# A decoder layer with 32 experts on one core: expert 1's tokens are gathered before expert 0's last weight unit, and the final norm's weight comes by a transfer

## The chip, the cores and the metric

The kernel runs on one core of one Trainium2 chip. The metric is the device time of one execution in microseconds (us); the kernel before has a median of 1227.49 us over 3 runs. The engines that matter here are TensorE (PE, matrix products), VectorE (DVE), ScalarE (ACT), GpSimd (POOL), and SyncE (SP), whose only work is to issue DMA transfers.

## The reference

One layer, 256 tokens of width 1024, all in float32. What lies before the experts (norm, projection, two kinds of attention, merge) is not touched by the change. The part that is:

```python
x = x + merged @ w_out[layer]
hf = rmsnorm(x, norm_ffn_g[layer])
x = x + moe_ffn(hf, w_router[layer], b_router[layer], w1[layer], b1[layer], w2[layer], b2[layer])
return rmsnorm(x, norm_final_g)

# moe_ffn: each token goes to the top 4 of 32 experts
gu = xb @ w1[e] + b1[e]                       # 1024 -> 2048
gate = jnp.minimum(gu[:, :F], SWIGLU_LIMIT)
up = jnp.clip(gu[:, F:], -SWIGLU_LIMIT, SWIGLU_LIMIT)
act = (up + 1.0) * gate * jax.nn.sigmoid(SWIGLU_ALPHA * gate)
y = act @ w2[e] + b2[e]                       # 1024 -> 1024, then weighed and added to the token
```

## The kernel before, in words

**Stages.** Up to about 309 us the kernel computes the attention part and the residual `x2`. Then it routes the tokens, and from about 320 us it walks through the 32 experts. Each expert has room for 64 tokens (`CAP`).

**One expert.** The weights of an expert arrive in six units of 2 MB: four of `w1` (two of eight rows of 128 each) and two of `w2`. For each expert PE *gathers* its tokens (48 small products of the token parts `x_parts` with a 0/1 selection, into PSUM bank 2, L1263, and 6 products that gather the tokens' norm scales into bank 3, L1251). DVE then multiplies the two into `XT` (`store_scales` L1814, `store_x` L1819). PE multiplies `XT` with the four `w1` units (`hidden_unit`, L1289), adds a bias (L1299), and the sums lie in banks 0 and 1. DVE and ACT make the activation of them (`activate`: clamps L1890 and L1891, sigmoid on ACT L914, products L1899 and L1902). PE transposes it (L1336), multiplies with the two `w2` units (L1355), and scatters the result into banks 4 to 7 (L1444), which hold the residual from the start. In the loop each of these steps belongs to another expert, so that PE needs not wait: expert i+1's hidden units, then the gather for i+2, the scatter for i, and the `w2` units of i. The transposes of expert i's activation (`transpose_previous`) come behind the first hidden unit of expert i+1.

**The weight stream.** SP issues the transfers in one fixed order into a ring of ten units. Before it issues unit n it waits until PE has used unit n-9 (`s_used`, counted up at the end of each unit). So PE gives back the places, and DMA fills them.

**Expert 0** stands apart, in `hidden_first`, ahead of the loop. Its order on PE: unit 0, unit 1, unit 2, bias, the scales of expert 1 (`second_scales`), then `spread_gain`, then unit 3. `spread_gain` (L1470) multiplies rows of the final norm's weight with columns of the identity, so that banks 6 and 7 hold this weight in all 128 partitions. ACT copies it to the tile `gain` (L907). That tile is also `rest`, scratch space of POOL and ACT while they split `x2` in three bf16 parts (until `s_lo` is 4), so the copy can't be earlier; and banks 6 and 7 must be free again before ACT puts the second half of the residual there (L910, `s_res`). Behind unit 3 PE gathers expert 1's tokens, runs 8 filler products (`fill(3, 8)`) and waits for the residual and for `XT`. It can't gather earlier, as `XT` is one tile: DVE may overwrite it with expert 1's tokens only when unit 3 has read expert 0's.

**The end.** Behind the last unit and the last scatter ACT sums squares (L942, L944), and DVE multiplies with the root and with `gain` (L1966, wait on `s_gain`) and SP stores the result (L633).

Of the kernel before, what the change touches and what calls it, by code (L numbers as in the profile page):

```python
# [7 lines left out]
ALU = mybir.AluOpType  # L8
# [101 lines left out]
def hybrid_block_kernel(nc, x_in, g_mix, w_in, rel_bias, w_att, w_ret, w_out, g_ffn, w_router, b_router,  # L110
                        w1, b1, w2, b2, g_final, c_early, c_lasting, c_decay, c_onehot, c_mask, c_item,
                        c_expert, out):
    with ExitStack() as ctx:
# [3 lines left out]
        def sem(name):  # L117
            return ctx.enter_context(nc.semaphore(name))
# [4 lines left out]
        def bank(b, n=1):  # L123
            return psf[:, b * HALF:(b + n) * HALF]
# [101 lines left out]
        ul = A_W[:, 5632:6144]  # L226
        sg = A_W[:, 6144:6656]
        act_sb = gl
        s_w = A_W[:, 6656:6912].rearrange("p (t s) -> p t s", t=TT)
        sc_w = A_W[:, 6912:7168]  # L230
        actT = A_W[:, 7168:7680]
# [147 lines left out]

        s_pair = [sem(f"ring_pair_loaded{j}") for j in range(RING // 2)]  # L380
        s_unit = [sem(f"w1_unit_of_first_or_last_or_extra_loaded{u}") for u in range(W1_UNITS)]
        s_gainp = sem("final_gain_in_psum")
        s_used = sem("ring_units_used")
        s_xfirst = sem("first_rows_of_first_tokens_stored")
        s_extra2 = [sem(f"extra_w2_loaded{u}") for u in range(W2_UNITS)]
# [133 lines left out]
        def _(sp):  # L519
# [96 lines left out]
            for j in range(W2_ROWS):  # L616
                flat = place(N_UNITS - 1)[0]
                sp.dma_start(w2_tile(flat)[:, j, :], w2_source(N_EXP - 1, 1)[:, j, :]).then_inc(s_quarter[j], 16)

            sp.wait_ge(s_used, N_UNITS)  # L620
            sp.wait_ge(s_table, 1)
            n = sp.value_load(list_i[0:1, 0:1], min_val=0, max_val=MAX_EXTRA)
# [15 lines left out]
        def _(pool):  # L638
# [34 lines left out]
            def low_part(m):  # L673
                t, h, cols = HALVES[(2, 3, 0, 1)[m]]
                pool.wait_ge(s_mid, m + 1)
                pool.tensor_tensor(x_part(2, t)[:, cols], rest[:, h], x_part(1, t)[:, cols], ALU.subtract)\
                    .then_inc(s_lo, 1)
# [16 lines left out]
            rest_part(1)  # L694
            low_part(2)
            low_part(3)
            pool.wait_ge(s_res, 2 * TT)
            pool.memset(sc_w, 0.0).then_inc(main.swe, 1)
            pool.memset(y_sb, 0.0).then_inc(main.ye, 1)

# [1 line left out]
        def _(act):  # L703
# [77 lines left out]
                          w_router.rearrange("(u p j) e -> p u j e", p=P, j=PAIR_ROWS)).then_inc(s_small, 16)  # L781
            act.dma_start(br_sb[:, :], bass.AP(b_router.tensor, 0, [[0, P], [1, N_EXP]])).then_inc(s_small, 16)
            act.dma_start(item_sb[:, :], c_item).then_inc(s_small, 16)
            act.dma_start(g_rows[:, :], g_final.rearrange("(c p) -> c p", p=P)).then_inc(s_grows, 16)
            act.dma_start(expert_sb[:, :], c_expert).then_inc(s_small, 16)
            with nc.allow_non_contiguous_dma(reason="1024 words, off the critical path"):
                act.dma_start(g_col[:, :].rearrange("p (u j) -> p u j", j=PAIR_ROWS),
# [112 lines left out]
            for t in range(TT):  # L900
                act.activation(gexp[:, t, :], top[:, 8 * t:8 * t + 4], ACT.Exp, bias=lowest[:, t, :],
                               accum_out=gden[:, t:t + 1]).then_inc(s_tke, 1)
            for t in range(TT):
                if t:
                    act.wait_ge(s_gainp, 1)
                    act.wait_ge(s_lo, 2 * TT)
                    act.activation(gain[:, :], bank(6, 2), ACT.Copy).then_inc(s_gain, 1)  # L907
                    act.wait_ge(s_gain, 1)
                for h in range(2):
                    act.activation(by_row_pair(bank(4 + 2 * t + h))[:, 0], in_row_pairs(x2[:, t, h * HALF:(h + 1) * HALF])[:, 0],  # L910
                                   ACT.Copy).then_inc(s_res, 1)
            def sigmoid(s, i):
                act.wait_ge(s.g, i + 1)
                act.activation(sg, gl, ACT.Sigmoid, scale=ALPHA).then_inc(s.sig, 1)  # L914
# [3 lines left out]
                act.activation(actT, bank(2), ACT.Copy).then_inc(s.ate, 1)  # L918

            act.activation(warm, warm, ACT.Sigmoid)  # L920
            sigmoid(main, 0)
            store_act(main, 0)
            with act.Fori(0, N_EXP - 2) as i:
                act.activation(warm, warm, ACT.Sigmoid)
# [24 lines left out]
        def _(pe):  # L949
# [330 lines left out]
                        scales.then_inc(main.gathered, 1)  # L1280
                mm.then_inc(main.gathered, 1)

            def hidden_unit(flat, u, row_done=None):
                tile = w1_tile(flat)
                for j in range(W1_ROWS):
                    k = u * W1_ROWS + j
                    for c in range(4):
                        o = ps[CAP * (c % 2):CAP * (c % 2) + CAP, c // 2, :]
                        mm = pe.matmul(o, XT[:, k, :], hidden_columns(tile[:, j, :], c),  # L1289
                                       start=(k == 0), stop=(k == KC - 1))  # L1290
                    if j == 0 and row_done is not None:
                        mm.then_inc(row_done, 1)
                return mm

            def hidden_bias(s, i):
                pe.wait_ge(s.sel1, i + 1)
                for c in range(4):
                    o = ps[CAP * (c % 2):CAP * (c % 2) + CAP, c // 2, :]
                    pe.matmul(o, sel1[0:BIAS_ROWS, :], hidden_columns(bias[:, 0:2 * F], c), start=False, stop=False)  # L1299

            def hidden_first():

                pe.wait_ge(s_xfirst, 1)
                for u in range(W1_UNITS):
                    pe.wait_ge(s_unit[u], 16)
                    if u == 1:
                        pe.wait_ge(main.x, 1)
                    hidden_unit(first_units[u], u, s_wu if u < HALF_UNITS else None).then_inc(s_used, 1)
                    if u == 2:
                        hidden_bias(main, 0)  # L1310
                        second_scales()
                        spread_gain()

            def hidden(i, first, rounds, behind_first_unit):

# [148 lines left out]
                pe.wait_ge(main.slots, 2)  # L1464
                gather_scales().then_inc(main.gathered, 1)

            def spread_gain():
                pe.wait_ge(s_grows, 32)
                for c in range(KC):
                    mm = pe.matmul(psf[:, 6 * HALF + c * P:6 * HALF + (c + 1) * P],  # L1470
                                   ident[0:KC, c:c + 1].broadcast_to([KC, P]), g_rows[:, :], start=(c % 4 == 0),
                                   stop=True, skip_group_check=True)
                mm.then_inc(s_gainp, 1)

            fill(0, 6)
            gather_first()
            fill(0, 6)
            pe.wait_ge(s_bias, 12)
            hidden_first()
            pe.wait_ge(s_lo, 2 * TT)  # L1480
            gather(main, 1, scaled=True)
            pe.wait_ge(main.scales, 2)
            fill(3, 8)
            pe.wait_ge(s_res, 2 * TT)
            with pe.Fori(0, (N_EXP - 2) // TURN) as r:
                rounds = r * (16 * TURN * E_UNITS // RING)
                for k in range(TURN):
# [28 lines left out]
        def _(dve):  # L1516
# [307 lines left out]
            for n, rows in enumerate((slice(0, W1_ROWS), slice(W1_ROWS, KC))):  # L1824
                count = rows.stop - rows.start
                scaled = dve.tensor_tensor(scale_rows[:, rows, :], scale_row.broadcast_to([P, count, CAP]),
                                           gain_of_row[:, rows, :], ALU.mult)
                if n:
                    scaled.then_inc(main.scales, 1)
                    dve.wait_ge(main.scales, 1)  # L1830
                else:
                    link(scaled)
                    dve.wait_ge(main.gathered, 2)
                dve.tensor_tensor(XT[:, rows, :], bank(2).rearrange("p (k s) -> p k s", k=KC)[:, rows, :],
                                  scale_rows[:, rows, :], ALU.mult).then_inc(main.x if n else s_xfirst, 1)
            choose_bias(sel1, main.sel1, 0)
            choose_bias(sel2, main.sel2, 0)
# [48 lines left out]
            def down_done(i):  # L1886
                dve.wait_ge(s_used, i * E_UNITS + W1_UNITS + E_UNITS)

            def activate(s, i, stored=None, scaled=False):
                dve.tensor_scalar(gl, bank(0), LIMIT, None, ALU.min).then_inc(s.g, 1)  # L1890
                dve.tensor_scalar(ul, bank(1), LIMIT, -LIMIT, ALU.min, ALU.max).then_inc(s.chain, 1)  # L1891
                if stored is not None and not scaled:
                    dve.wait_ge(s.x, stored)
                    store_scales(s, stored, scale_rows)
                dve.wait_ge(s.chain, i * 2 + 1)
                dve.wait_ge(s.g, i + 1)
                if stored is not None:
                    store_x(s, stored, scale_rows)
                dve.scalar_tensor_tensor(ul, ul, 1.0, gl, ALU.add, ALU.mult).then_inc(s.chain, 1)  # L1899
                dve.wait_ge(s.chain, i * 2 + 2)  # L1900
                dve.wait_ge(s.sig, i + 1)
                dve.tensor_tensor(act_sb.rearrange("s (j p) -> s j p", j=W2_ROWS),  # L1902
                                  ul.rearrange("s (p j) -> s j p", j=W2_ROWS),
                                  sg.rearrange("s (p j) -> s j p", j=W2_ROWS), ALU.mult).then_inc(s.act, 1)
# [5 lines left out]
                dve.wait_ge(s.sw, i + 1)  # L1910
                dve.tensor_copy(sc_w, ps[:, 2, 0:T]).then_inc(s.swe, 1)

            dve.wait_ge(s_res, 2 * TT)
            store_scales(main, 1, scale_rows)
            dve.wait_ge(s_used, W1_UNITS)
            activate(main, 0, 1, scaled=True)
            choose_bias(sel1, main.sel1, 1)
            slots(main, 2, 2)
            with dve.Fori(0, N_EXP - 2) as i:
                gated_slots(main, i, i, i)  # L1920
                hidden_done(i + 1)
                activate(main, i + 1, i + 2)
                choose_bias(sel1, main.sel1, i + 2)
                slots(main, i + 3, i + 3)
                store_scatter(main, i)
                down_done(i)
                store_y(main, i)
                choose_bias(sel2, main.sel2, i + 1)
# [13 lines left out]
            with dve.If(n > 0):  # L1942
# [15 lines left out]
                    store_y(extra, i)  # L1958
                dve.wait_ge(s_scattered, n + N_EXP + 1)
                dve.memset(lists[0:1, 64:65], 0.0)  # L1960
            dve.wait_ge(s_gain, 1)
            for n, (t, h, cols) in enumerate(HALVES):
                if h == 0:
                    dve.wait_ge(s_root, TT + t + 2)
# [33 lines left out]
```

## Time and profile before

| | us |
|---|---|
| median of 3 runs (lowest 1227.3, highest 1229.3) | 1227.49 |
| the profiled execution | 1227.92 |
| its span | 1225.9 |
| PE busy | 1169.0 (95%) |
| DVE busy | 428.0 (35%) |
| ACT busy | 207.7 (17%) |
| POOL busy | 58.5 (5%) |

The span is the time from the first to the last instruction of the profiled execution; what lies around it is 1227.92 - 1225.9 = 2.02 us. DMA moved 461.79 MB, 377 GB/s over the span. The granted clock of PE was 0.999 of full speed. PE is busy nearly all the time, but it isn't the only limit: the slices of the page show that DMA is at 400 GB/s and more over two thirds of the span.

### The profile page before, as it was taken

Reading aid. Unit: us, or ns where it says so; the run is one execution under the profiler, and the core shown is the slowest. Engines: PE = TensorE matmul, PEld = TensorE weight load, DVE = VectorE, ACT = ScalarE, POOL = GpSimd, SP = SyncE. Lnnn points to the kernel's source line nnn. Section 1 sums busy time; section 2 is a strip of 40 time slices with the busy share of each in tenths; the row PEclk is TensorE's granted clock in tenths of the full one; section 3 lists DMA queues with packets and bytes.
Section 4 is the critical chain, followed back from the end, with each engine's and each line's share of the span. In section 5 each row is a group of like instructions: output and inputs, shape, how many; then the busy total and the mean of one; then the engine's idle time right before and its main releaser. Section 6 shows DMA issues by size and latency. Waiting matters only on the chain.

```text
span 1225.9 us, 17199 instructions
## 1 busy us (share of the span) xinstructions
PE 1169.0 (95%) x7154; PEld 588.0 (48%) x7154; DVE 428.0 (35%) x741; ACT 207.7 (17%) x306; POOL 58.5 (5%) x43
## 2 busy tenths in 40 slices
PE   9999999999999999999999999999999899999897
PEld 8888888888643334333333333333333333333332
DVE  5886764655632223222222222222222222222222
ACT  6444553534400000000000000000000000000001
POOL 0850000000300000000000000000000000000000
PEclk9999999999999999999999999999999999999999
DMA  9756437877889999999999999999999999999996
GB/s 310 272 207 217 161 138 258 317 283 320 337 350 428 431 433 433 429 431 434 433 430 430 433 433 432 429 433 434 432 429 433 433 433 428 433 433 434 428 423 255
DMA packets 47522, 461.79 MB, mean 377 GB/s; under 512 B 4985, under 2 KB 6978, under 8 KB 32290
## 3 DMA queue, kind: packets, MB, share of 16 engines
q1 hardware_dynamic: 44760, 458.97, 89.9%
q10 hardware_dynamic: 2730, 2.36, 0.7%
q8 instruction: 24, 0.39, 0.1%
q14 instruction: 8, 0.07, 0.0%
HBM read 459.19 MB, written 1.07 MB: 375 GB/s over the span
## 4 chain that ended last, share of the span: by engine, by line
PE 66%; DMA 32%; DVE 1%; SPq 1%; ACT 0%; issue 0%; DVEq 0%; ACTq 0%
PE ps L1289 19%; DMA w_ring<-in_w 19%; PE ps L1355 12%; DMA A_QK<-in_w 6%; DMA xb_and_att<-in_w 6%; PE ps L1006 4%; PE ps L1444 4%; PE ps L1014 3%; PE ps L1012 3%; PE ps L1013 3%; PE ps L1263 2%; PE ps L1007 2%; PE ps L1026 1%; PE ps L1139 1%; PE ps L1141 1%; PE ps L1140 1%
## 5 line engine op out<-in xcount | busy, mean ns | idle before, releaser
L1289 PE MATMUL ps<-w_ring,A_W 128*64 128x512 f32 x1216 | 272.5, 596 | 28.9 <-DMA w_ring<-in_w 28.4
L1890 DVE TENSOR_SCALAR A_W<-ps 128x512 f32<-128x512 f32 x32 | 22.1, 692 | 478.2 <-PE ps L1289 478.2
L1289 PEld LDWEIGHTS ps<-w_ring,A_W 128*64 128x64 f32 x1216 | 84.8, 137 | 200.9 <-issue 160.2
L1355 PE MATMUL ps<-w_ring,A_W 128*64 128x512 f32 x608 | 137.9, 595 | 0.0
L1534 DVE TENSOR_TENSOR w_parts<-w_ring,w_parts 128x1024 fp32r<-128x1024 f32 x76 | 109.9, 1463 | 56.4 <-ACT w_parts L733 55.5
L1289 PE MATMUL ps<-A_QK,A_W 128*64 128x512 f32 x416 | 93.2, 595 | 9.3 <-DMA A_QK<-in_w 9.3
L918 ACT ACTIVATE A_W<-ps 128x512 f32<-128x512 f32 x31 | 18.5, 597 | 462.9 <-PE ps L1336 462.9
L1289 PE MATMUL ps<-xb_and_att,A_W 128*64 128x512 f32 x384 | 86.2, 596 | 9.4 <-DMA xb_and_att<-in_w 9.4
L733 ACT ACTIVATE w_parts<-w_ring 128x1024 fp32r<-128x1024 f32 x75 | 78.9, 1058 | 64.6 <-PE ps L1007 32.1
L914 ACT ACTIVATE A_W<-A_W 128x512 f32<-128x512 f32 x32 | 20.2, 631 | 359.8 <-DVE A_W L1890 359.8
L1006 PE MATMUL ps<-hT_both,w_parts 128*128 128x512 f32 x224 | 79.3, 399 | 0.0
L1355 PEld LDWEIGHTS ps<-w_ring,A_W 128*64 128x64 f32 x608 | 41.5, 136 | 70.5 <-issue 69.0
L1012 PE MATMUL ps<-w_parts,hT_both 128*128 128x512 f32 x176 | 69.6, 396 | 0.0
L1014 PE MATMUL ps<-w_parts,hT_both 128*128 128x512 f32 x176 | 68.6, 390 | 0.0
L1013 PE MATMUL ps<-w_parts,hT_both 128*128 128x512 f32 x176 | 68.5, 389 | 0.0
L1444 PE MATMUL ps<-A_W 64*128 64x512 f32 x264 | 65.9, 616 | 0.0
L1007 PE MATMUL ps<-hT_both,w_parts 128*128 128x256 f32 x224 | 62.9, 281 | 0.0
L1289 PEld LDWEIGHTS ps<-A_QK,A_W 128*64 128x64 f32 x416 | 29.3, 137 | 68.1 <-issue 59.7
L1289 PEld LDWEIGHTS ps<-xb_and_att,A_W 128*64 128x64 f32 x384 | 26.3, 137 | 64.3 <-issue 47.8
L1907 DVE COPY A_W<-ps 128x512 f32<-128x512 f32 x31 | 21.4, 692 | 98.0 <-PE ps L1355 98.0
L1263 PE MATMUL ps<-route,x_parts 128*128 128x64 bf16 x1488 | 48.5, 193 | 0.0
L1006 PEld LDWEIGHTS ps<-hT_both,w_parts 128*128 128x128 f32 x224 | 42.1, 188 | 11.1 <-issue 0.6
(266 smaller groups left out, 1198.7 us busy)
## 6 DMA issues: line engine op xcount, KB each, us to landing
w_ring<-in_w SPq DMA_DIRECT2D x110, 2048.0 KB, 35.2
A_QK<-in_w SPq DMA_DIRECT2D x38, 2048.0 KB, 35.1
xb_and_att<-in_w SPq DMA_DIRECT2D x35, 2048.0 KB, 35.2
w_ring<-in_w_in SPq DMA_DIRECT2D x36, 1024.0 KB, 7.3
w_ring<-in_w SPq DMA_DIRECT2D x8, 1024.0 KB, 23.7
w_ring<-in_w_ret_branch SPq DMA_DIRECT2D x2, 2048.0 KB, 10.9
xb_and_att<-in_w SPq DMA_DIRECT2D x4, 1024.0 KB, 20.6
A_W<-in_w_out SPq DMA_DIRECT2D x1, 2560.0 KB, 13.0
```

The costliest lines, as they stand in the source:

```text
L733: act.activation(hi, raw, ACT.Copy).then_inc(s_wh, 1)
L1006: pe.matmul(o, wh, tokens_both(k), start=first, stop=False, skip_group_check=True)
L1007: mm = pe.matmul(o[:, 0, :], wl, hT_hi[:, k, :], start=False, stop=last, skip_group_check=True)
L1012: pe.matmul(bank(b + t), hh, hi, start=first, stop=False)
L1013: pe.matmul(bank(b + t), hh, lo, start=False, stop=False)
L1014: mm = pe.matmul(bank(b + t), hl, hi, start=False, stop=last)
L1263: mm = pe.matmul(ps[:, 2, k * CAP:(k + 1) * CAP], row_columns(x_part(part, t), k), s_one[:, t, :], start=(part == 0 and t == 0), stop=(par ...
L1289: mm = pe.matmul(o, XT[:, k, :], hidden_columns(tile[:, j, :], c), start=(k == 0), stop=(k == KC - 1))
L1355: mm = pe.matmul(ps[CAP * c:CAP * c + CAP, 3, :], lhs, w2_tile(flat)[:, q % W2_ROWS, c * HALF:(c + 1) * HALF], start=False, stop=(q == FQ ...
L1444: mm = pe.matmul(bank(4 + 2 * t + c), weights[rows, t * P:(t + 1) * P], y[rows, :], start=False, stop=True, skip_group_check=True)
L1534: dve.tensor_tensor(lo, raw, hi.bitcast(F32), ALU.subtract).then_inc(s_wl, 1)
L1890: dve.tensor_scalar(gl, bank(0), LIMIT, None, ALU.min).then_inc(s.g, 1)
```

## The change

1. The sums of expert 0's hidden layer go to banks 6 and 7 (`FIRST_BANK = 6`) instead of 0 and 1, and its tokens lie in `XT_first`, which is the place of `gl`, instead of `XT`.
2. PE gathers expert 1's tokens before unit 3 of expert 0. DVE stores its scales and its tokens at once, without waiting for the residual, and chooses bias and slots of the experts that follow before it clamps expert 0's sums.
3. `spread_gain` and its row transfer go. SP loads `gain` with one transfer of 128 copies of the row (512 KB), issued behind the last weights.
4. The filler products behind expert 0 go. ACT puts the second half of the residual in banks 6 and 7 after the sigmoid of expert 0, when DVE has read both banks. PE no longer waits for the residual; DVE does before it enters its loop. POOL clears `sc_w` one step earlier.

```diff
+        XT_first = gl.rearrange("p (k s) -> p k s", k=KC)
+        FIRST_BANK = 6
...
@@ sync, behind the last w2 quarter
+            sp.wait_ge(s_lo, 2 * TT)
+            sp.dma_start(gain[:, :], bass.AP(g_final.tensor, 0, [[0, P], [1, D]])).then_inc(s_gain, 16)
             sp.wait_ge(s_used, N_UNITS)
@@ gpsimd
+            pool.wait_ge(s_res, 2)
+            pool.memset(sc_w, 0.0).then_inc(main.swe, 1)
             pool.wait_ge(s_res, 2 * TT)
-            pool.memset(sc_w, 0.0).then_inc(main.swe, 1)
             pool.memset(y_sb, 0.0).then_inc(main.ye, 1)
@@ scalar
-            act.dma_start(g_rows[:, :], g_final.rearrange("(c p) -> c p", p=P)).then_inc(s_grows, 16)
...
-            for t in range(TT):
-                if t:
-                    act.wait_ge(s_gainp, 1)
-                    act.wait_ge(s_lo, 2 * TT)
-                    act.activation(gain[:, :], bank(6, 2), ACT.Copy).then_inc(s_gain, 1)
-                    act.wait_ge(s_gain, 1)
+            def store_residual(t):
                 for h in range(2):
                     act.activation(by_row_pair(bank(4 + 2 * t + h))[:, 0], in_row_pairs(x2[:, t, h * HALF:(h + 1) * HALF])[:, 0],
                                    ACT.Copy).then_inc(s_res, 1)
+            store_residual(0)
...
             act.activation(warm, warm, ACT.Sigmoid)
+            act.wait_ge(s_res, 2)
             sigmoid(main, 0)
+            act.wait_ge(main.chain, 1)
+            store_residual(1)
+            act.wait_ge(s_res, 2 * TT)
             store_act(main, 0)
@@ tensor (hidden_unit and hidden_bias take the first bank, b, and hidden_unit the tokens, x)
-                    hidden_unit(first_units[u], u, s_wu if u < HALF_UNITS else None).then_inc(s_used, 1)
+                    hidden_unit(first_units[u], u, s_wu if u < HALF_UNITS else None, FIRST_BANK, XT_first).then_inc(s_used, 1)
                     if u == 2:
-                        hidden_bias(main, 0)
+                        hidden_bias(main, 0, FIRST_BANK)
                         second_scales()
-                        spread_gain()
+                        pe.wait_ge(s_lo, 2 * TT)
+                        gather(main, 1, scaled=True)
...
             hidden_first()
-            pe.wait_ge(s_lo, 2 * TT)
-            gather(main, 1, scaled=True)
-            pe.wait_ge(main.scales, 2)
-            fill(3, 8)
-            pe.wait_ge(s_res, 2 * TT)
@@ vector
-                dve.tensor_tensor(XT[:, rows, :], bank(2).rearrange("p (k s) -> p k s", k=KC)[:, rows, :],
+                dve.tensor_tensor(XT_first[:, rows, :], bank(2).rearrange("p (k s) -> p k s", k=KC)[:, rows, :],
...
-            dve.wait_ge(s_res, 2 * TT)
+            dve.wait_ge(main.x, 1)
             store_scales(main, 1, scale_rows)
-            dve.wait_ge(s_used, W1_UNITS)
-            activate(main, 0, 1, scaled=True)
+            store_x(main, 1, scale_rows)
+            dve.wait_ge(s_used, W1_UNITS - 1)
             choose_bias(sel1, main.sel1, 1)
             slots(main, 2, 2)
+            dve.wait_ge(s_used, W1_UNITS)
+            activate(main, 0, b=FIRST_BANK)
+            dve.wait_ge(s_res, 2 * TT)
             with dve.Fori(0, N_EXP - 2) as i:
...
-            dve.wait_ge(s_gain, 1)
+            dve.wait_ge(s_gain, 16)
```

PE around expert 0, before. `A_ATT`, `w_ring` and `A_W` hold the four weight units, `x_parts` the tokens to be gathered, `ones_bf` is the filler.

```order
L1289 MATMUL ps<-A_ATT,A_W 64x512 x8
L1289 MATMUL ps<-w_ring,A_W 64x512 x16
L1299 MATMUL ps<-bias_sb,route 64x512 x4
L1251 MATMUL ps<-route,small 128x64 x6
L1470 MATMUL ps<-g_rows,lasting 128x128 x8
L1289 MATMUL ps<-A_W 64x512 x8
L1263 MATMUL ps<-route,x_parts 128x64 x48
L1197 MATMUL ps<-ones_bf 128x128 x8
```

And now:

```order
L1293 MATMUL ps<-A_ATT,A_W 64x512 x8
L1293 MATMUL ps<-w_ring,A_W 64x512 x16
L1303 MATMUL ps<-bias_sb,route 64x512 x4
L1255 MATMUL ps<-route,small 128x64 x6
L1267 MATMUL ps<-route,x_parts 128x64 x48
L1293 MATMUL ps<-A_W 64x512 x8
```

The eight products with `g_rows` and the eight fillers are gone, and the 48 of the gather stand ahead of unit 3; the loop follows directly behind it.

DVE at the same place, before. L1814 and L1819 store the scales and tokens of expert 1; L1890, L1891, L1899 and L1902 are the activation of expert 0; L1805 and L1800 choose bias and slots.

```order
L1814 TENSOR_TENSOR A_W<-ps,g_col 128x512
L1890 TENSOR_SCALAR A_W<-ps 128x512
L1891 TENSOR_SCALAR A_W<-ps 128x512
L1819 TENSOR_TENSOR A_W<-ps,A_W 128x512
L1899 SCALAR_TENSOR_TENSOR A_W<-A_W 128x512
L1902 TENSOR_TENSOR A_W<-A_W 128x512
L1805 TENSOR_SCALAR route<-lasting 96x64
L1800 TENSOR_SCALAR route<-lasting,A_PT 128x64 x2
```

And now:

```order
L1806 TENSOR_TENSOR A_W<-ps,g_col 128x512
L1811 TENSOR_TENSOR A_W<-ps,A_W 128x512
L1797 TENSOR_SCALAR route<-lasting 96x64
L1792 TENSOR_SCALAR route<-lasting,A_PT 128x64 x2
L1882 TENSOR_SCALAR A_W<-ps 128x512
L1883 TENSOR_SCALAR A_W<-ps 128x512
L1891 SCALAR_TENSOR_TENSOR A_W<-A_W 128x512
L1894 TENSOR_TENSOR A_W<-A_W 128x512
```

The tokens of expert 1 are stored ahead of the activation of expert 0 instead of in its middle, and so are the choices of bias and slots.

ACT at the same place, before: the residual's first half (L910), the copy of the gain (L907), the residual's second half, the load of the sigmoid's table, the sigmoid (L914), the store of the transposed activation (L918).

```order
L910 ACTIVATE ps<-A_W 128x2x128x2 x2
L907 ACTIVATE gain<-ps 128x1024
L910 ACTIVATE ps<-A_W 128x2x128x2 x2
L920 ACT_TABLE_LOAD
L920 ACTIVATE small<-small 128x1
L914 ACTIVATE A_W<-A_W 128x512
L918 ACTIVATE A_W<-ps 128x512
```

And now:

```order
L908 ACTIVATE ps<-A_W 128x2x128x2 x2
L920 ACT_TABLE_LOAD
L920 ACTIVATE small<-small 128x1
L914 ACTIVATE A_W<-A_W 128x512
L908 ACTIVATE ps<-A_W 128x2x128x2 x2
L918 ACTIVATE A_W<-ps 128x512
```

The residual's second half now stands between the sigmoid and the store.

## Rows read from the trace of the kernel before

**Rows 1.** The page's 40 slices of 30.6 us: DMA's rate.

```profile
GB/s 310 272 207 217 161 138 258 317 283 320 337 350 428 431 433 433 429 431 434 433 430 430 433 433 432 429 433 434 432 429 433 433 433 428 433 433 434 428 423 255
```

**Rows 2.** The chain of waits from 331 us: start, duration, what ran.

```profile
331.40 1.98 PE ps L1470 x16
333.38 3.58 PE ps L1289 x16
336.96 1.52 PE ps L1263 x48
...
338.61 0.70 DVE A_W L1819
...
339.45 3.65 PE ps L1289 x16
343.10 0.45 PE ps L1299 x4
```

**Rows 3.** Windows: stretch, length, busy time of PE, PEld, DVE, ACT, POOL, clock, DMA share, GB/s.

```profile
324.00:339.50 15.50, 14.97 (x132) 7.77 (x129) 9.77 (x34) 7.40 (x14) 2.58 (x4) 1.00 0.98 395
339.50:344.00 4.50, 4.50 (x24) 1.70 (x24) 2.46 (x7) 0.00 (x0) 0.00 (x0) 1.00 0.01 5
344.00:1211.00 867.00, 819.94 (x5214) 303.18 (x5212) 201.34 (x430) 42.98 (x96) 0.00 (x0) 1.00 1.00 430
```

**Rows 4.** The timeline of SP's issues from 330 us: start, time, line.

```profile
330.70 0.33 SPq L597 DMA_DIRECT2D w_ring<-in_w  x1
343.14 4.96 SPq L442 DMA_DIRECT2D w_ring<-in_w  x2
```

**Rows 5.** The chain of waits at one turn of PE's loop, and from 602 us on.

```profile
467.32 3.58 PE ps L1355 x16
470.90 3.43 PE ps L1289 x16
...
602.97 36.85 DMA w_ring<-in_w
...
1125.38 38.94 DMA xb_and_att<-in_w
...
1164.36 7.09 PE ps L1289 x32
...
1211.49 5.30 PE ps L1404 x24
...
1220.50 1.41 DVE xb L1966 x2
```

**Rows 6.** The timeline of DVE, POOL and ACT, 323 to 341 us.

```profile
323.71 2.15 DVE L1800 TENSOR_SCALAR route<-lasting,A_PT 128x64 bf16<-128x64 f32 x2
324.66 1.15 POOL L676 TENSOR_TENSOR x_parts<-gain,x_parts 128x512 bf16<-128x512 f32 x1
332.06 0.16 DVE L1873 CAST wr_sb<-wr_sb 1x16 int32<-1x16 f32 x1
334.47 1.12 ACT L910 ACTIVATE ps<-A_W 128x512 f32<-128x512 f32 x2
335.68 0.69 DVE L1814 TENSOR_TENSOR A_W<-ps,g_col 128x512 f32<-128x512 f32 x1 [3.46 <-ACT ps L910]
337.62 0.68 DVE L1891 TENSOR_SCALAR A_W<-ps 128x512 f32<-128x512 f32 x1
337.74 0.63 ACT L914 ACTIVATE A_W<-A_W 128x512 f32<-128x512 f32 x1 [0.63 <-DVE A_W L1890]
339.22 0.68 DVE L1899 SCALAR_TENSOR_TENSOR A_W<-A_W 128x512 f32<-128x512 f32 x1
339.93 1.07 DVE L1902 TENSOR_TENSOR A_W<-A_W 128x512 f32<-128x512 f32 x1
```

**Rows 7.** Windows at the end of the weight stream; the page's issues of `x`, KB each, us to landing.

```profile
1212.50:1213.00 0.50, 0.50 (x5) 0.14 (x2) 0.00 (x0) 0.00 (x0) 0.00 (x0) 1.00 0.10 41
xb<-in_x SPq DMA_DIRECT2D x4, 512.0 KB, 4.2
```

More of the change, by code:

```diff
@@ L381, in hybrid_block_kernel @@
         s_unit = [sem(f"w1_unit_of_first_or_last_or_extra_loaded{u}") for u in range(W1_UNITS)]
-        s_gainp = sem("final_gain_in_psum")
         s_used = sem("ring_units_used")
@@ L1281, in gather_first, with hidden_unit @@
                 mm.then_inc(main.gathered, 1)
-            def hidden_unit(flat, u, row_done=None):
+            def hidden_unit(flat, u, row_done=None, b=0, x=XT):
                 tile = w1_tile(flat)
@@ L1287, in hidden_unit @@
                     for c in range(4):
-                        o = ps[CAP * (c % 2):CAP * (c % 2) + CAP, c // 2, :]
-                        mm = pe.matmul(o, XT[:, k, :], hidden_columns(tile[:, j, :], c),
+                        o = ps[CAP * (c % 2):CAP * (c % 2) + CAP, b + c // 2, :]
+                        mm = pe.matmul(o, x[:, k, :], hidden_columns(tile[:, j, :], c),
                                        start=(k == 0), stop=(k == KC - 1))
@@ L1293, in hidden_unit, with hidden_bias @@
                 return mm
-            def hidden_bias(s, i):
+            def hidden_bias(s, i, b=0):
                 pe.wait_ge(s.sel1, i + 1)
                 for c in range(4):
-                    o = ps[CAP * (c % 2):CAP * (c % 2) + CAP, c // 2, :]
+                    o = ps[CAP * (c % 2):CAP * (c % 2) + CAP, b + c // 2, :]
                     pe.matmul(o, sel1[0:BIAS_ROWS, :], hidden_columns(bias[:, 0:2 * F], c), start=False, stop=False)
@@ L1465, in second_scales @@
                 gather_scales().then_inc(main.gathered, 1)
[L1467 to L1473, printed above, removed]
             fill(0, 6)
@@ L1887, in down_done, with activate @@
                 dve.wait_ge(s_used, i * E_UNITS + W1_UNITS + E_UNITS)
[L1889 to L1892, printed above, removed]
+            def activate(s, i, stored=None, b=0):
+                dve.tensor_scalar(gl, bank(b), LIMIT, None, ALU.min).then_inc(s.g, 1)
+                dve.tensor_scalar(ul, bank(b + 1), LIMIT, -LIMIT, ALU.min, ALU.max).then_inc(s.chain, 1)
+                if stored is not None:
                     dve.wait_ge(s.x, stored)
```

## The prediction

> **What bounds the kernel now.** I read the page's slices first, then the chain of waits, then windows around the first experts and at the end. The slices show three parts [rows 1]. Up to about 368 us DMA moves less than its best, 138 to 350 GB/s. From slice 13 to the last but one it stays at 423 to 434 GB/s, which is all that it reaches anywhere. A stream that is always full can't be shortened by making PE faster inside it. It can only be started earlier. So the question is where its last hole lies, and what ends it.
>
> The windows answer that [rows 3]. From 324 to 339.5 us the DMA share is 0.98. From 339.5 to 344.0 it is 0.01, a hole of 4.5 us less a last rest. From 344.0 to 1211.0 us it is 1.00 at 430 GB/s, without any hole. SP's issues say why [rows 4]: after the issue at 330.70 comes the next at 343.14, and that is the transfer which waits for PE's fifth used unit, the first hidden unit of expert 1. In the chain of waits this unit runs from 339.45 for 3.65 us, until 343.10 [rows 2]. The first bytes of the full stream move about 0.9 us behind the issue.
>
> Behind it the chain is PE alone until about 602 us and then alternates between transfers of 36.85 to 38.94 us and PE [rows 5]. That is the same stream seen from two sides: PE, which had a lead of some units, has used them up. The last wait for weights ends at 1164.36, and from there PE runs to the end. So everything from 344 to the end hangs on one time, the end of the first hidden unit of expert 1. What PE saves before it, up to the size of the hole, comes out at the end in full; what it saves behind it would not.
>
> **The change part by part.**
>
> *Spreading the gain on PE.* The chain gives it 1.98 us, 331.40 to 333.38, with PE the only engine in it and nothing beside it that PE would otherwise wait for [rows 2]. It goes: -1.98 us.
>
> *The gather before unit 3.* The gather costs 1.52 us wherever it stands (336.96 to 338.48 [rows 2]): 0 by itself. What changes is the stretch behind it. Now DVE starts on the tokens only when the gather ends (L1819, 338.61, 0.70 us), and hidden unit 0 of expert 1 begins at 339.45 [rows 2]. Between 338.48 and 339.45 PE runs only fillers or waits: 0.97 us. In the new order DVE does this beside unit 3. With the gain gone the gather runs from 331.40 to 332.92, unit 3 from there for 3.58 us to 336.50. DVE is ready for it: its work on the routing tables ends at 332.06 + 0.16 = 332.22, then the scales take 0.69 us and the tokens 0.70 us, so `XT` is there at about 333.9, 2.6 us before PE wants it [rows 2, 6]. The gather's own inputs are there too, though PE asks for them 5.6 us sooner than before: the low parts at 324.66 + 1.15 = 325.81, the slots at 323.71 + 2.15 = 325.86 [rows 6], against 331.40. So the stretch of 0.97 us goes: -0.97 us. In the kernel before, the scales waited for the residual (3.46 us idle, released by ACT's L910 [rows 6]); that wait goes with it, and cost PE nothing.
>
> *The entry into PE's loop.* The branch stood behind fillers and a wait of PE; now it follows unit 3 directly, with nothing between. At a turn of the loop the trace shows no gap: the down unit at 467.32 takes 3.58 us, and the next hidden unit starts at 470.90 [rows 5]. The first entry is another matter, since its code may not be there yet, and the trace hides it. It costs at least 0 and at most about the idle part of the 0.97 us, some 0.5 us. It is nearest to the loop's turn, so I take 0 and keep 0.5 for the range.
>
> *The activation of expert 0.* It is the new tight place. PE transposes the activation after one hidden unit and a bias, 3.65 + 0.45 = 4.10 us after hidden unit 0 begins [rows 2], and it now begins when unit 3 ends, 2.49 us sooner than before (339.45 - 336.96). Counted from the end of unit 3, DVE did the clamps until 338.30, at 1.34 us; then it waited for the gather and stored the tokens; then it did L1899 in 0.68 us and L1902 in 1.07 us [rows 6]. Without the tokens between: 1.34 + 0.68 + 1.07 and 0.1 between them = 3.19 us. The sigmoid is off this path, as it ended at 338.37, or 1.41 us [rows 6]. So it is ready 0.91 us before PE asks. The residual's second half (1.12 us on ACT [rows 6]) stands behind the sigmoid and delays neither it nor the products; it ends at about 1.41 + 1.12 = 2.5 us, and the store of the transposed activation comes behind the transposes at 4.10. Cost 0; if ACT's copies and DVE slow each other, up to 0.91 us is covered.
>
> *The places in PSUM and SBUF.* The products have the same shapes in other banks: 0. ACT's copy of the gain and the row transfer issued on ACT's queue were covered by waits of ACT: 0. POOL's clear of `sc_w` comes earlier, and was not late.
>
> *The gain's transfer.* It is issued on SP behind the last weights, and behind it SP has only the final stores. The weight stream ends at about 1213.0 (window 1212.5 to 1213.0, share 0.10 [rows 7]), and `gain` is first read at 1220.50 [rows 5]. Both move together. 512 KB took a median of 4.2 us from issue to landing for `x` [rows 7], and at 430 GB/s [rows 3] it takes 1.2 us of the stream. So it lands between 1214.2 and 1217.2 in the old clock, at least 3.3 us before it is wanted. The last weights are ahead of it in the queue, and the end of PE's last stretch starts at 1211.49 with 5.30 us of products [rows 5], so a slight overlap with the last quarter would not be felt either. Cost 0. A source of which one row is read 128 times is not in the trace; that is the second rival.
>
> A rule of the Trainium skill bears on it ("DMA: Bandwidth & Descriptors", section "Rules for kernel authors"): a leading zero-stride dimension of c copies confines a transfer to at most c engines, for c below 16. Here c is 128, so by the rule all 16 engines are used and the cost is 0 as taken; no row here shows such a transfer of this size.
>
> **The sum.** -1.98 - 0.97 = -2.95 us for the start of the first hidden unit of expert 1, so for SP's issue (343.14 to 340.19) and for the stream's start (344.0 to about 341.05). The old transfers still end at about 339.6, so the hole shrinks from about 4.4 to 1.45 us and doesn't close: none of the gain is cut off. By the profiled execution: 1227.92 - 2.95 = 1224.97 us. Its time is 0.43 above the median of the runs, so against the median 1227.49 it is 1224.54; I say 1224.6.
>
> **The rivals.**
>
> *Part of it is taken back at expert 1's start.* The first entry of the loop costs up to 0.5 us, or the activation comes later than the 0.91 us of cover, for instance by contention in PSUM between ACT's residual copy and DVE. For it: the cover is thin and nothing in the trace shows that entry uncovered. Against it: the sum above has every step from a row. Price 0.5 to 1.4 us: 1225.1 to 1226.0.
>
> *The transfer of the gain is late.* One mechanism: its 128 reads of one row run on one or few of the 16 engines, or are served one after the other. On one engine the 512 KB at 430 / 16 = 27 GB/s take 19.5 us, from about 1212.5 to 1232 in the old clock instead of 1220.5, so +11.5 - 2.95 = +8.6 us: about 1236. It decides from 1220.5 on, that is if it takes over 7.5 us, and is slower than before if it takes over 10.5 us. Against it: 128 partitions are written, as with `x`, whose 512 KB landed in 4.2 us.
>
> *The stream doesn't pass it on.* If DMA isn't the full stream that its share claims, the saved time could be lost at a later hole, and the time stays 1227.5. For it: only that 350 to 340 GB/s slices stand close by. Against it: share 1.00 over 867 us, and in that span PE's chain would move by the same 2.95 us too. The nearest thing to it is a slower rate after a longer queue, which no row shows.
>
> **How the numbers follow.** Forecast as summed, 0.73: 1224.0 to 1225.1 with the runs' own spread. Part taken back, 0.17. Not passed on, 0.06. Gain late, 0.04, of which nearly all is slower. About 0.2% (2.45 us) is what a measurement of this kernel can tell from no change; the forecast of 2.95 us is only 0.5 us beyond it, and the runs before spread over 2 us. So of the forecast's 0.73 I count 0.62 as faster and 0.11 as the same; with part taken back (0.02 faster, 0.15 same) and not passed on (0.05 same, 0.01 slower): faster 0.64, same 0.31, slower 0.05. The range holds the forecast and most of the first rival: 1223.5 to 1226.3.
>
> **What would show it.** In the profile after, the chain should have no g_rows products, the gather at about 331.4, unit 3 ending at about 336.5, hidden unit 0 of expert 1 starting there without idle time, the transposes at about 340.6 without a wait for DVE, SP's next issue at about 340.2, a hole in DMA of about 1.5 us, then share 1.00; the last wait for weights should end at about 1161.4, and the span should be about 1222.9. The forecast is wrong if PE waits between unit 3 and the loop, or in front of the transposes, if the last wait for weights moves by less than 2.4 us, or if the first of the final products waits for a transfer.

## The result, and the profile after

The changed kernel takes 1233.28 us (median of 6 runs, 1233.01 to 1233.74), the kernel before 1227.45 us in the same comparison. The ratio is 1.0044, with a 95% interval of 1.0032 to 1.0056: slower by 5.8 us, where 2.95 us less were forecast. The profiled execution took 1233.71 us, its span is 1231.7 us.

The start went as forecast. Here is the chain of waits after, from 331 us, and SP's issue that opens the full weight stream (compare [rows 2, 4]):

```profile
331.08 1.40 PE ps L1267 x48
332.48 7.02 PE ps L1293 x32
339.50 0.45 PE ps L1303 x4
```

```profile
339.54 4.95 SPq L443 DMA_DIRECT2D w_ring<-in_w  x2
```

Unit 3 of expert 0 and the first hidden unit of expert 1 are now one piece of 32 records without a gap, and SP issues at 339.54 instead of 343.14: 3.60 us sooner. The loss is behind it. The chain at the first turn of PE's loop, to be read beside 467.32 and 470.90 of [rows 5]:

```profile
463.71 3.58 PE ps L1360 x16
467.30 3.84 issue
471.14 1.97 PE ps L1293 x4
473.11 3.84 issue
476.95 4.55 PE ps L1293 x12
```

PE stands still twice, for 3.84 us each, and the profile knows nothing that it waits for ("issue"). Two such stalls, of 3.0 to 4.7 us, return at each of the five turns (the branches back; the loop runs six times). Here is PE's idle time before L1293 that is put down to issue, from the list of waits (total, times, longest; ten of the eleven times are those at the turns), and the instruction queue on the page (packets, MB, share of 16 engines):

```profile
PE ps L1293 <- issue: 38.0, 11, 4.7
```

```profile
q8 instruction: 69, 1.13, 0.4%
```

The same row on the page of before:

```profile
q8 instruction: 24, 0.39, 0.1%
```

Between 470 and 1180 us the trace of before has no packet on this queue at all, and the trace after has 44. Here is the queue of the weights (q1) in this stretch, before, and then the queues of weights and instructions after:

```profile
q1 hardware_dynamic: 11798, 306.44, 100.3%
```

```profile
q1 hardware_dynamic: 11710, 304.47, 99.9%
q8 instruction: 44, 0.72, 0.4%
```

An instruction packet is 1.13 MB / 69 = 16 KB. The last wait for weights ends at 1170.16 instead of 1164.36 [rows 5], though the stream began 3.60 us sooner; so the stream lost 9.4 us on its way:

```profile
1131.18 38.93 DMA xb_and_att<-in_w
...
1170.16 7.09 PE ps L1293 x32
```

From there to the end both kernels need the same 61.54 us (1231.7 - 1170.16 and 1225.9 - 1164.36), so the tail with the gain's transfer cost nothing. And this is how the stream ends (windows of 1 us; the last two columns are DMA's share and GB/s), first before, then after:

```profile
1208.00:1209.00 1.00, 1.00 (x10) 0.46 (x10) 0.94 (x2) 0.00 (x0) 0.00 (x0) 1.00 1.03 410
1211.00:1212.00 1.00, 1.00 (x8) 0.29 (x6) 0.00 (x0) 0.00 (x0) 0.00 (x0) 1.00 0.50 197
1212.00:1213.00 1.00, 1.00 (x8) 0.34 (x6) 0.00 (x0) 0.00 (x0) 0.00 (x0) 1.00 0.18 74
```

```profile
1208.00:1209.00 1.00, 1.00 (x8) 0.25 (x4) 0.98 (x1) 0.00 (x0) 0.00 (x0) 1.00 0.97 397
...
1212.00:1213.00 1.00, 1.00 (x8) 0.35 (x6) 0.00 (x0) 0.69 (x2) 0.00 (x0) 1.00 0.50 205
1216.00:1217.00 1.00, 1.00 (x6) 0.30 (x4) 0.00 (x0) 0.00 (x0) 0.00 (x0) 1.00 0.52 213
1218.00:1219.00 1.00, 1.00 (x8) 0.30 (x6) 0.00 (x0) 0.00 (x0) 0.00 (x0) 1.00 0.27 111
```

For 9 us after, the share is one half and the rate one half; before, the end takes about 3 us in all. I read this as half of the 16 engines having finished while the other half lag behind; the trace doesn't name the engine of a packet.

### The profile page after: what moved, and what is told of

Same layout as the page of the kernel before. It is cut to its first block, busy times and chain, and to the rows that moved or that the text cites. A ratio compares the mean times of both kernels' runs of the same rounds, so it can differ in the third digit from the quotient of the medians.

```text
span 1231.7 us, 17151 instructions
## 1 busy us (share of the span) xinstructions
PE 1175.6 (95%) x7130; PEld 592.7 (48%) x7130; DVE 427.2 (35%) x741; ACT 206.6 (17%) x305; POOL 58.1 (5%) x43
## 3 DMA queue, kind: packets, MB, share of 16 engines
q8 instruction: 69, 1.13, 0.4%
HBM read 459.71 MB, written 1.07 MB: 374 GB/s over the span
## 4 chain that ended last, share of the span: by engine, by line
PE 83%; DMA 12%; issue 3%; DVE 0%; ACT 0%; SPq 0%; DVEq 0%; POOL 0%; ACTq 0%; POOLq 0%
PE ps L1293 32%; PE ps L1360 14%; DMA w_ring<-in_w 9%; PE ps L1010 4%; PE ps L1449 4%; PE ps L1018 3%; PE ps L1016 3%; PE ps L1017 3%; DMA xb_and_att<-in_w 3%; PE ps L1267 3%; PE ps L1011 2%; PE ps L1341 1%; PE ps L1303 1%; PE ps L1030 1%; PE ps L1143 1%
## 5 line engine op out<-in xcount | busy, mean ns | idle before, releaser
L1293 PE MATMUL ps<-w_ring,A_W 128*64 128x512 f32 x1216 | 285.3, 617 | 44.3 <-issue 37.8
L1293 PEld LDWEIGHTS ps<-w_ring,A_W 128*64 128x64 f32 x1216 | 90.4, 141 | 221.5 <-issue 212.9
L1360 PE MATMUL ps<-w_ring,A_W 128*64 128x512 f32 x608 | 137.9, 595 | 0.0
L918 ACT ACTIVATE A_W<-ps 128x512 f32<-128x512 f32 x31 | 18.5, 597 | 492.4 <-PE ps L1341 492.4
L1293 PE MATMUL ps<-A_QK,A_W 128*64 128x512 f32 x416 | 92.8, 594 | 0.0
L1293 PE MATMUL ps<-xb_and_att,A_W 128*64 128x512 f32 x384 | 85.9, 595 | 3.4 <-DMA xb_and_att<-in_w 3.4
L914 ACT ACTIVATE A_W<-A_W 128x512 f32<-128x512 f32 x32 | 20.2, 631 | 343.3 <-DVE A_W L1882 343.3
L1360 PEld LDWEIGHTS ps<-w_ring,A_W 128*64 128x64 f32 x608 | 41.5, 136 | 70.5 <-issue 69.0
L1293 PEld LDWEIGHTS ps<-A_QK,A_W 128*64 128x64 f32 x416 | 29.3, 137 | 57.1 <-issue 57.1
L1899 DVE COPY A_W<-ps 128x512 f32<-128x512 f32 x31 | 21.4, 692 | 98.0 <-PE ps L1360 98.0
L1293 PEld LDWEIGHTS ps<-xb_and_att,A_W 128*64 128x64 f32 x384 | 26.8, 137 | 56.8 <-issue 50.7
```

The source lines that it names most:

```text
L1293: mm = pe.matmul(o, x[:, k, :], hidden_columns(tile[:, j, :], c), start=(k == 0), stop=(k == KC - 1))
L1360: mm = pe.matmul(ps[CAP * c:CAP * c + CAP, 3, :], lhs, w2_tile(flat)[:, q % W2_ROWS, c * HALF:(c + 1) * HALF], start=False, stop=(q == FQ ...
```

## The experiments

**a1: the changed kernel, its loop put back in its place.**

```diff
-            keep_busy(51)
+            keep_busy(27)
+            for _ in range(48):
+                pe.matmul(ps[:, 1, 0:P // 2], ones_bf[:, :], ones_bf[:, 0:P // 2], start=True, stop=True)
```

> The changed kernel with 24 more warm-up products on PE at the very start (75 instead of 51; 48 of them have 64 columns, so that all together still stream the columns of 51). They add 48 instructions, as many as the change took away in front of PE's loop, so that the loop's code stands where it stood in the kernel before. Theory of the fetch (the loop of 1738 instructions no longer fits PE's instruction memory after a shift of 48, and is fetched again at each turn): no idle time marked issue at a turn, 24 packets on the instruction queue instead of 69, granted clock back at 0.999, the start gained by the change (3.6 us in one profile) comes out at the end: 1223.5 to 1224.5 us. Rival (the new order itself, the residual copied late, the sums in banks 6 and 7 or the gain's transfer slow the loop or the stream): nothing changes, about 1233.3 us.

Measured: 1224.03 us (6 runs), ratio to before 0.9966 (0.9954 to 0.9979), clock 0.999. Its page and chain:

```profile
q8 instruction: 24, 0.39, 0.1%
```

```profile
1121.74 38.94 DMA xb_and_att<-in_w
...
1160.73 7.09 PE ps L1295 x32
```

```profile
1208.00:1209.00 1.00, 1.00 (x6) 0.29 (x4) 0.00 (x0) 0.00 (x0) 0.00 (x0) 1.00 0.72 287
1209.00:1210.00 1.00, 1.00 (x8) 0.30 (x6) 0.00 (x0) 0.00 (x0) 0.00 (x0) 1.00 0.39 160
1212.00:1213.00 1.00, 1.00 (x6) 0.14 (x2) 0.00 (x0) 0.00 (x0) 0.00 (x0) 1.00 0.00 0
```

No stall, no lagging half, and the last wait for weights ends 3.63 us before that of the kernel before: the gain of the start (3.60 us in the profile after), passed on in full. The rival, that the new order itself is slow, falls.

**a2: the kernel before, its loop moved as the change moves it.**

```diff
-            keep_busy(51)
+            keep_busy(3)
+            for _ in range(24):
+                pe.matmul(ps[:, 1, 0:2 * P].rearrange("p (a e) -> p a e", a=2), ones_bf[:, :],
+                          ones_bf[:, :].rearrange("p (a e) -> p a e", a=1).broadcast_to([P, 2, P]), start=True, stop=True)
```

> The kernel before with nothing of the change, but 24 warm-up products fewer at the very start (27 instead of 51; 24 of them have 256 columns, so that the same columns are streamed). This moves PE's loop 48 instructions forward, as the change did. Theory of the fetch: two stalls of 3 to 4 us marked issue at each of the five turns of PE's loop, 69 packets on the instruction queue, clock about 0.978, and 9.4 us lost in the weight stream: about 1236.9 us. Rival (the new order itself is slow): within 0.5 us of the kernel before, 1227.5.

Measured: 1236.69 us, ratio 1.0068 (1.0052 to 1.0083), clock 0.981, 69 packets. In its chain:

```profile
470.51 3.06 issue
473.56 1.08 PE ps L1292 x4
474.64 4.47 issue
```

So the place of the code alone, with none of the change's work, costs 9.2 us.

**a3: the gain by transfer alone.** `spread_gain`, its load and ACT's copy go, SP's transfer comes, and 16 added warm-up products keep the loop in its place.

```diff
+            sp.wait_ge(s_lo, 2 * TT)
+            sp.dma_start(gain[:, :], bass.AP(g_final.tensor, 0, [[0, P], [1, D]])).then_inc(s_gain, 16)
...
-                        spread_gain()
```

> The kernel before with one part of the change alone: the products that spread the final norm's weight are gone, and the weight comes by the transfer behind the last weights; the gather, the fillers and the order of DVE and ACT stay. 16 more warm-up products of 2 instructions each (67 instead of 51, the same columns in all) keep the loop's code in its place. By the prediction's first term: 1.98 us less, 1225.5 us, with the final products waiting for no transfer. If the transfer is late or disturbs the last weights: 1227.5 or more. Theory of the fetch: no stalls at the turns, since the code isn't moved.

Measured: 1225.66 us (11 runs), ratio 0.9979 (0.997 to 0.9988): 1.8 us less. The first term of the prediction holds, and the tail waits for no transfer. The rest of a1's gain, 1225.66 - 1224.03 = 1.6 us, is left for the gather's new place and the order that comes with it; that part was not run alone, and a difference of two medians is known to about 1 us only.

**a4: the stall alone, on the kernel before.** PE's loop stands at the start of a block, and PE waits at each turn for a chain of memsets on GpSimd.

```diff
+            pool.wait_ge(s_lg, TT)
+            pool.memset(wr_sb[:, 4:8, :], 0.0).then_inc(s_delay, 1)
+            pool.wait_ge(s_delay, 1)
+            for q in range((N_EXP - 2) // TURN):
+                pool.wait_ge(s_used, q * (TURN * E_UNITS) + W1_UNITS + TURN * E_UNITS)
+                for n in range(28):
+                    pool.wait_ge(s_step, q * 28 + n)
+                    pool.memset(wr_sb[:, 4:8, :], 0.0).then_inc(s_step, 1)
+                pool.wait_ge(s_step, q * 28 + 28)
+                pool.memset(wr_sb[:, 4:8, :], 0.0).then_inc(s_delay, 1)
+                pool.wait_ge(s_delay, q + 2)
...
+            pe.addr_align(256, offset=0, max_nops=0)
             with pe.Fori(0, (N_EXP - 2) // TURN) as r:
+                pe.wait_ge(s_delay, r + 1)
```

> The kernel before with PE's loop placed at the start of a fetch block, so that it fits, and PE made to wait at each turn until GpSimd has run a chain of 29 small memsets (about 8 us) that starts when PE has used the turn's last unit. No instruction is fetched again; only the stall of the changed kernel's turns is copied, at one piece. If the stall is what the weight stream loses time by: about 9 us more than the kernel before, 1236. If the ring's queued transfers cover the stall, and the fetched packets take the time from the stream: up to 1 us more than before.

Measured: 1232.31 us, ratio 1.0035 (1.0022 to 1.0048), clock 0.98, and between what either theory expected. The waits of PE, SP's first issue of the stream, and the last wait for weights:

```profile
PE ps L1302 <- POOL wr_sb L711: 39.8, 5, 8.1
```

```profile
346.35 4.96 SPq L444 DMA_DIRECT2D w_ring<-in_w  x2
```

```profile
1168.43 6.65 PE ps L1302 x29
```

The stream started 346.35 - 343.14 = 3.21 us late, before any turn. Two things made it late. One is the entry into the loop: PE idled 2.41 us in front of it for no reason that the profile knows, where it idled 0.53 us before. The other is that PE ran unit 3 of expert 0 in 5.35 us instead of 3.65, as the granted clock stood at 0.50, though PE had been busy without a break for over 10 us. (1.88 + 1.70 us, less 0.37 us by which this profile was ahead, makes the 3.21.)

```profile
332.94 5.35 PE L1302 MATMUL ps<-A_W 128*64 128x512 f32 x16
...
342.66 3.65 PE L1302 MATMUL ps<-w_ring,A_W 128*64 128x512 f32 x16 [2.41 <-issue]
```

```profile
335.00:337.00 2.00, 2.00 (x6) 0.49 (x4) 0.69 (x1) 1.71 (x3) 0.92 (x3) 0.50 1.01 426
```

The last wait ended 1168.43 - 1164.36 = 4.07 us late. The five stalls of 8 us and the slow clock behind them account for at most the 0.86 us between.

**b1 and b2: how sharp the bound is.** The changed kernel with `pe.addr_align(256, offset=40, max_nops=0)` in front of the loop, and with `offset=64`.

Measured, one run each: 1223.55 us with slot 40, 1233.21 us with slot 64. The queue on the page of the first, then of the second, and the second's waits of PE:

```profile
q8 instruction: 24, 0.39, 0.1%
```

```profile
q8 instruction: 69, 1.13, 0.4%
```

```profile
PE ps L1293 <- issue: 17.0, 6, 3.7
```

With the same work and the same code, 24 slots decide 9.7 us. The bound lies between slots 40 and 64, as the count says (1792 - 1738 = 54). I had expected two stalls at each turn of b2, and there is one: 17.0 us in all, less than half of the changed kernel's 38.0. The clock is 0.991 instead of 0.978. But the packets are the same 69, and so is the time. What PE stalls less in b2 it waits more for weights. Its waits for those of the ring, first in the changed kernel and then in b2:

```profile
PE ps L1293 <- DMA w_ring<-in_w: 6.5, 6, 1.4
```

```profile
PE ps L1293 <- DMA w_ring<-in_w: 21.4, 15, 2.8
```

So the time goes with the packets, and not with the length of the stalls. (In b2's profile the stream lost 8.7 us: it began at 339.71 and the last wait ended at 1169.65. Between profiles this loss differs by some 0.7 us.)

**b3: a prefetch hint for the branch back.**

```diff
-            with pe.Fori(0, (N_EXP - 2) // TURN) as r:
+            with nc.Fori(0, (N_EXP - 2) // TURN, engines=OrderedEngineSet([pe.engine]), hint_back_edge=True) as r:
```

> The changed kernel, with its loop where it is, and a prefetch hint for PE's branch back at the end of the loop (one instruction more in the loop). The packets should stay near 69, the stalls at the turns shrink or go. Theory that the packets cost the most (they take their time from the weight stream; the copied stall alone cost under 2 us): 1231 to 1233 us even without stalls. If the stalls cost the most: near 1224 to 1226 us.

Measured: 1224.1 us, ratio 0.9971 (0.996 to 0.9983). My expectation missed: not only the stalls went, the packets did too.

```profile
q8 instruction: 24, 0.39, 0.1%
```

So it doesn't tell packets from stalls, but it is a remedy that needs no count of slots. The traces hint at how it works. These are the packets from 330 to 465 us, the first pass through the loop, in b4 (the next run, whose loop needs no hint) and then in b3:

```profile
q8 instruction: 7, 0.11, 0.3%
```

```profile
q8 instruction: 6, 0.10, 0.3%
```

From 1175 us on, behind the loop, it is the other way round, 3 packets in b4 and 4 in b3, and in between neither has any. So with the hint one block is not fetched ahead on the way through the loop but after it. That fits the 45 packets more over five turns of the changed kernel, which are 9 a turn: 8 blocks that the loop touches and one behind it. My reading is that PE keeps eight blocks and fetches the one behind the loop too, so that a loop over eight blocks pushes out its own first one, unless the hint holds that fetch back. It fits the packets of every run here; no run tested it by itself.

**b4: the loop at the start of a block.** `pe.addr_align(256, offset=0, max_nops=0)`.

> The changed kernel with PE's loop placed at the start of a block of 256 instructions, as a remedy that doesn't depend on the code in front of it. Theory of the fetch: no stalls at the turns, 24 or 25 packets, 1224.0 us as with the 24 added products, plus the entry over the padding: at most 47 slots of padding here, so I expect 0 to 1 us.

Measured: 1224.15 us, ratio 0.997 (0.9958 to 0.9981), 24 packets. SP's first issue of the stream is at 339.91, so the short padding cost at most 0.4 us.

**c1: the stall again, on b4.** The memset chain of a4 in the kernel of b4.

> The changed kernel with its loop at the start of a block (1224.15 us in its own run, 24 packets) and the chain of GpSimd memsets of the earlier stall run, so that PE stalls about 8 us at each of the five turns and nothing is fetched again. In the earlier run the first transfer behind the start came 3.2 us late (the entry over about 230 slots of padding), which hides what the stalls cost; here the entry was free. If the packets are the cause: at most 1.5 us above 1224.15. If the stalls cost what the changed kernel lost: 1233.

Measured: 1229.3 us (11 runs, 1227.53 to 1230.73), which is 5.1 us over b4 and outside what I expected of the packets. The trace says that my edit was at fault: the first release by GpSimd stands behind its wait for the residual, which the changed kernel puts in later, and PE waited 3.47 us for it in front of the loop. Behind this wait the granted clock fell to 0.50, and the first hidden unit took 5.35 us instead of b4's 3.60.

```profile
339.66 5.35 PE L1306 MATMUL ps<-w_ring,A_W 128*64 128x512 f32 x16 [3.47 <-POOL wr_sb L707]
```

```profile
341.00:343.00 2.00, 2.00 (x8) 0.75 (x6) 0.00 (x0) 0.00 (x0) 0.00 (x0) 0.50 0.00 0
```

```profile
345.04 4.96 SPq L445 DMA_DIRECT2D w_ring<-in_w  x2
```

```profile
PE ps L1306 <- POOL wr_sb L715: 40.5, 5, 8.1
```

```profile
1130.59 35.05 DMA xb_and_att<-in_w
1165.68 7.09 PE ps L1306 x32
```

The stream began 345.04 - 339.91 = 5.13 us after that of b4 and the last wait ended 1165.68 - 1160.66 = 5.02 us after. The five stalls of 40.5 us in all added nothing, though the clock was 0.979 as in the changed kernel. The transfer of 35.05 us, instead of 38.94 in a1, shows where a stall goes: the queue in front of DMA gets shorter, and it never ran empty, as DMA's share stayed at 1.00 from 470 to 1180 us.

## Why the prediction was wrong

- **The gain's products, -1.98 us.** Right: a3 measured -1.8 us.
- **The stretch behind the gather, -0.97 us.** Right in kind and a little small. All of it came, and the pieces run faster without a break: from the end of the scales to the end of the first hidden unit it is 8.42 us now (331.08 to 339.50) and was 11.70 us (331.40 to 343.10), 3.28 us less instead of 2.95. The rest of the 3.60 us is in the part ahead of it, where profiles of the same code differ by some 0.3 us. Here, too, the prediction's entry into the loop cost nothing: PE goes from unit 3 into the loop without a gap (332.48 7.02 PE ps L1293 x32).
- **The activation's cover, 0.91 us.** Right: it ended at 338.16 + 1.07 = 339.23 and was wanted at 339.95, 0.72 us of cover.

```profile
338.16 1.07 DVE L1894 TENSOR_TENSOR A_W<-A_W 128x512 f32<-128x512 f32 x1
```

- **The gain's transfer, 0.** Right: the final products waited for ACT only, and the tail took 61.54 us as before. The rule on zero-stride sources of the Trainium skill ("DMA: Bandwidth & Descriptors", section "Rules for kernel authors") gave the same.
- **The entry into PE's loop, 0 with 0.5 kept.** This step failed, not in its 0 for the first entry but in what it rests on. I read 467.32 to 470.90 [rows 5], no gap at a turn, as a property of the loop, and so put the turns at nothing. It is a property of the loop at one place in the instruction blocks. The missing term is: 48 instructions fewer in front of the loop, so the loop is fetched again at five turns. It measured +9.2 us (a2 against before) and +9.25 us (the changed kernel against a1).
- **What PE saves before the stream comes out at the end.** Right for what it was said of: a1 has -3.4 us. But "a stream that is always full" was not the same as one that carries only weights. DMA's share stayed at 1.00 in the changed kernel; part of it was instructions.

So of the prediction's rivals the third ("the stream doesn't pass it on", 0.06) named the right place, but its price was no gain at all, and the stream lost 5.8 us more than that. The second (the gain's transfer late, 1236 us) came near the measured 1233.28 us in its number only: a1 and a3 have the same transfer and no such loss.

Of the 9.4 us that the stream lost, the stalls are under 1 us (a4, c1), and b2 shows it from the other side. The rest goes with the packets. The windows at the stream's end show how, by my reading: half of the engines are 9 us behind. PE waits for the whole of a transfer, so a load on some engines delays each transfer by the whole of their lag. The bytes agree: from 470 to 1180 us the changed kernel moved 306.44 - 304.47 = 1.97 MB of weights less than the kernel before, 4.6 us at 430 GB/s, and it would be 4.7 us if half of the engines lose 9.4 us and the other half nothing. If the packets all go to that half, 69 - 24 = 45 more of them at 9.4 us are 9.4 x 8 / 45 = 1.7 us of an engine for each 16 KB. The packets themselves took about 1.0 us each (0.4% of 16 engines over 710 us, for 44 packets); at the stream's rate (430 / 16 = 27 GB/s for an engine) their bytes alone would be 0.6 us. These are estimates. What the other 0.7 us is, and which engines carry the packets, the trace doesn't show. I haven't tried packets without stalls.

The first rival (part taken back at the loop's entry, 0.5 to 1.4 us) came near the place with a size far too small, and it looked at the first entry alone. The page of before bears the clue: 24 packets on the instruction queue, by an estimate about as many as PE's program has blocks, and none of them between 470 and 1180 us, so each block was fetched once, though the loop ran six times. That said that the loop fits; how nearly it fills the room, only the count says. The Trainium skill ("Runtime: NRT & Kernel Launch", section "Instruction fetch mechanics") gives PE 2048 instructions in blocks of 256, that is 8; 1738 instructions lie in 7 or 8 of them, by their place. The runs agree with the size of a block (16 KB a packet) and, without the hint of b3, with a bound where the loop comes to touch an eighth block. The same section of the Trainium skill says that a taken branch to a block outside the current window of two must wait for a fetch. The stalls at the turns after agree with the wait, but not with a window of two: in the kernel before, PE branches back over 6.8 blocks five times without a gap and without a packet, and the measurement decides.

The best version is the changed kernel with its loop placed: 1224.03 (a1), 1224.15 (b4) or 1224.1 us (b3), 0.3% under the kernel before.

## What to carry to other kernels

Before you cost an edit in front of a long loop, look at the row of the instruction queue: if the loop's code is fetched only once, ask how near it is to no longer fitting, and count how far the edit moves it. Place such a loop, or give its branch back a hint, and then measure the edit. And when a stream of transfers is the bound, look at what else rides on its engines, since a few small packets on some of them can delay every transfer.

## What the runs showed that I had not expected

- 24 slots of one instruction (slot 40 against slot 64) changed the time by 9.7 us, in a kernel of 1224 us.
- Forty us of stalls on PE, busy at 95%, cost less than 1 us, as the ring's queue in front of DMA took them; 0.74 MB of instructions in 463 MB cost over 8.
- The entry over some 230 slots of padding (by the count) went with 2.4 us of idle time in front of the loop (a4), over at most 47 with 0.4 us or less (b4).
- The granted clock fell to half (0.5, the 1.2 GHz level instead of 2.4, in windows of 4 us behind each turn) when PE had idled for 7 to 8 us in two pieces, and over the whole run to 0.978; in b2, with shorter stalls, it was 0.991. The time followed neither. In a4 it fell to half once with no idle time of PE ahead of it.
